# One form of d and the sum S4 moved one product later, and two blocks' rows normalised in other units

## The reference

```python
u = (x @ w_in).reshape(b, t, 4, 256)                  # four groups of 256 features
pooled[g] = trailing mean of u[:, :, g] over (2, 4, 8, 16)[g] rows
y = einsum('btgc,gce->btge', pooled - u, w_group) * scale
m = y @ w_out
h = layer_norm(ALPHA * x + m, ln_mix_g, ln_mix_b)
gate, up = split(h @ w_gu)                            # 2 x 2816 columns
h = layer_norm(ALPHA * h + (silu(gate) * up) @ w_down, ln_ffn_g, ln_ffn_b)
return h without the meta rows
```

## Time and profile before

| what | us |
|---|---|
| median of three executions | 1663.8 |
| the profiled execution | 1664.46 |
| its span | 1662.6 |
| TensorE busy in matmuls | 1643.4 |
| VectorE busy | 1040.2 |
| GpSimd busy | 649.1 |
| ScalarE busy | 616.8 |

### The profile page before, as it was taken

One profiled execution on the slowest core, in us unless ns is written; L12 is line 12 of the kernel. 1 busy time (PEld: TensorE's weight loads), 2 busy tenths in 40 slices (PEclk: granted clock), 3 DMA queues, 4 the chain that ended last, 5 costly groups with the idle time before them and its releaser, 6 DMA issues.

```text
span 1662.6 us, 19027 instructions
## 1 busy us (share of the span) xinstructions
PE 1643.4 (99%) x7302; PEld 1358.0 (82%) x7302; DVE 1040.2 (63%) x1085; ACT 616.8 (37%) x836; POOL 649.1 (39%) x440
## 2 busy tenths in 40 slices
PE   9999999999999999999999999999999999999998
PEld 7888888787788888888888888888888888888886
DVE  6788785987444544345756676676554434368866
ACT  5335465446333333433533333333333322222320
POOL 0330025015346767665356656666621000341002
PEclk9999999999999999999999999999999999999999
DMA  9774477535356566576556667666668443564542
GB/s 350 253 284 152 160 254 259 187 127 194 122 164 208 188 201 222 184 228 213 202 181 204 214 219 221 202 190 198 203 190 302 170 161 126 195 216 177 199 144 94
DMA packets 190954, 330.84 MB, mean 199 GB/s; under 512 B 8464, under 2 KB 132496, under 8 KB 181136
## 3 DMA queue, kind: packets, MB, share of 16 engines
q1 hardware_dynamic: 151168, 297.64, 52.3%
q10 hardware_dynamic: 37520, 23.60, 4.6%
q0 software_dynamic: 2176, 8.39, 1.3%
HBM read 227.36 MB, written 102.24 MB: 198 GB/s over the span
## 4 chain that ended last, share of the span: by engine, by line
PE 90%; DVE 3%; POOL 2%; DMA 2%; ACT 1%; issue 1%; SPq 0%; POOLq 0%; DVEq 0%; ACTq 0%
PE acc L1231 43%; PE acc L1260 19%; PE turn L1231 7%; PE acc L1066 7%; PE turn L1260 6%; PE acc L1100 5%; PE turn L1100 3%; DMA hf_dram<-ss_mix 1%; POOL ss_mix L885 1%; DMA raw<-w_out 1%; DVE split L1653 1%; DVE sums L1698 1%; PE acc L1143 1%; PE turn L1054 0%; POOL ss_mix L931 0%
## 5 line engine op out<-in xcount | busy, mean ns | idle before, releaser
L1231 PE MATMUL acc<-fa,wf 128*128 128x512 f32 x1584 | 369.5, 393 | 5.4 <-DVE acc L1951 4.0
L1231 PE MATMUL acc<-fb,wf 128*128 128x512 f32 x1584 | 363.2, 389 | 0.2 <-DVE acc L1951 0.2
L1231 PEld LDWEIGHTS acc<-fa,wf 128*128 128x128 f32 x1584 | 298.0, 189 | 68.4 <-DVE wf L1827 5.1
L1231 PEld LDWEIGHTS acc<-fb,wf 128*128 128x128 f32 x1584 | 297.1, 188 | 62.7 <-issue 1.1
L1260 PE MATMUL acc<-dw,da 128*128 128x512 f32 x1386 | 315.3, 389 | 0.0
L1260 PEld LDWEIGHTS acc<-dw,da 128*128 128x128 f32 x1386 | 260.1, 188 | 54.0
L1827 DVE TENSOR_TENSOR wf<-wt,wf 128x512 fp32r<-128x512 f32 x132 | 133.7, 1014 | 164.8 <-ACT wf L1432 164.7
L885 POOL TENSOR_TENSOR wt<-wr,wt 128x512 f32<-128x512 f32 x88 | 137.7, 1565 | 174.5 <-DVE wf L1827 174.5
L1827 DVE TENSOR_TENSOR wf<-wr,wf 128x512 fp32r<-128x512 f32 x176 | 171.8, 980 | 52.7 <-ACT wf L1432 52.2
L1432 ACT CAST wf<-wr 128x512 fp32r<-128x512 f32 x176 | 108.6, 618 | 214.1 <-PE acc L1231 208.6
L1066 PE MATMUL acc<-mov,split 128*128 128x512 f32 x768 | 177.5, 391 | 0.0
(11 more groups left out here) (139 smaller groups left out, 1807.1 us busy)
## 6 DMA issues: line engine op xcount, KB each, us to landing
wr<-w_gu SPq DMA_DIRECT2D x44, 1024.0 KB, 5.1
dar<-af_dram SPq DMA_DIRECT2D x56, 704.0 KB, 4.3
af_dram<-g ACTq DMA_DIRECT2D x32, 512.0 KB, 5.5
raw<-w_in SPq DMA_DIRECT2D x15, 1024.0 KB, 7.0
fs<-hf_dram SPq DMA_DIRECT2D x14, 1024.0 KB, 5.6
dt_raw<-w_down SPq DMA_DIRECT2D x22, 512.0 KB, 5.9
wt_dram<-dt_t SPq DMA_DIRECT2D x22, 512.0 KB, 3.6
sa<-af_dram SPq DMA_DIRECT2D x22, 512.0 KB, 8.0
```

Of the source, the lines that this page charges most:

```text
L1231: mm = nc.tensor.matmul(dst, wf[:, slot, a, k, :], fa[half][i][:, v, :, k, :], start=i < 2 and k == 0 and n3 == 0, stop=k == KC - 1 and n3 ...
```

## The change

Form 1 of d gets its low part (`d_lo(h, 1)`) behind the split of product 1's weights and no longer in chunk 2 of the half's second block. S4 is made once, over the full tile, in `d_sums(h, 3)`, and no longer in two halves, so that `sd_made` counts seven in a half. Two waits keep `d11` and `d12` until their forms' low parts are made. Of block 2, rows 2 and 3 are normalised in unit 0, behind the `s5` copy. Of block 3, rows 2 and 3 are normalised in unit 2, rows 0 and 1 in unit 3, and stored at n = 3 and 4 of SyncE's list. `load_tform(0, 0)` waits for the stores of rows 2 and 3 alone. `norm` waits for `shift_ready` at each call.

```diff
@@ -323,6 +323,9 @@
         def mov_of(b):
             return mov[b in (1, 2)]
 
+
+        LAST_ROWS = (2, 3, 0, 1)
+
         def raw_d(b, i):
 
             q = ((d11, d12), (d21, d22))[b % 2][i // 2]
@@ -333,7 +336,7 @@
 
         FORM_D = (d11, d12, d11, d21, d12, e3, d22)
 
-        FORM_SUMS = (0, 0, 7, 6, 8, 2, 0)
+        FORM_SUMS = (0, 0, 6, 5, 7, 2, 0)
         FORM_GROUPS = (2, 4, 0, 0, 0, 0, 8)
         A_BANK = (acc[:, 4, :], acc[:, 5, :], turn[:, 0, :], turn[:, 1, :])
         B_BANK = tuple(acc[:, m, :] for m in range(TT))
@@ -351,7 +354,7 @@
 
         def form_ready(eng, h, t):
             if FORM_SUMS[t]:
-                eng.wait_ge(sd_made, 8 * h + FORM_SUMS[t])
+                eng.wait_ge(sd_made, 7 * h + FORM_SUMS[t])
             else:
                 eng.wait_ge(d_ready, 2 * PAIRS * h + FORM_GROUPS[t])
 
@@ -502,7 +505,7 @@
                 sp.dma_start(zm[e][:, j, :], x_rows[:, b * TT + j, :]).then_inc(z_landed[e][j], 16)
 
             def store_h(b, j):
-                sp.wait_ge(normed, b * TT + (j + 1))
+                sp.wait_ge(normed, b * TT + (LAST_ROWS.index(j) if b == LAST else j) + 1)
                 sp.dma_start(h_rows[:, b * TT + j, :], zm[b % 2][:, j, :]).then_inc(rows_stored[b % 2][j], 16)
 
             def load_ft(k):
@@ -539,7 +542,7 @@
                     sp.wait_ge(tf_made[e], 4 * v)
                 elif e == 0:
 
-                    for j in range(TT):
+                    for j in LAST_ROWS[0:2]:
                         sp.wait_ge(rows_stored[1][j], 2 * 16)
                 else:
 
@@ -800,9 +803,9 @@
                     load_a22()
                 if n % 2 == 0 and jj - 1 >= JF:
                     store_s(jj - 1 - JF)
-                if n in (1, 2):
-                    store_h(LAST, 2 * (n - 1))
-                    store_h(LAST, 2 * (n - 1) + 1)
+                if n in (3, 4):
+                    for j in LAST_ROWS[2 * (n - 3):2 * (n - 2)]:
+                        store_h(LAST, j)
                 for e in range(2):
                     if n - 1 in TF_STEP[e]:
                         store_tform(e, TF_STEP[e][n - 1])
@@ -1408,7 +1411,7 @@
                 elif i == 2:
 
                     act.wait_ge(d_lo_ready, NP * LAST_HALF + 4)
-                    act.wait_ge(sd_made, 8 * (LAST_HALF + 1))
+                    act.wait_ge(sd_made, 7 * (LAST_HALF + 1))
                 elif i < 5:
                     act.wait_ge(d_lo_ready, NP * LAST_HALF + (6 if i == 3 else NP))
                 elif i == 5:
@@ -1433,8 +1436,7 @@
                                ).then_inc(wf_hi, 1)
 
             def norm(s, j):
-                if j == 0:
-                    act.wait_ge(shift_ready, s + 1)
+                act.wait_ge(shift_ready, s + 1)
                 zz = zm[s % 2][:, j, :]
                 nc.scalar.activation(zz, zz, ACT.Identity, bias=shift[:, j:j + 1],
                                      scale=rstd[:, j:j + 1]).then_inc(normed, 1)
@@ -1498,7 +1500,7 @@
                         for q in range(4):
                             unit_hi(0, q)
                     if t == NP - 1:
-                        for j in range(TT):
+                        for j in range(TT if h == 0 else 2):
                             norm(2 * h, j)
                     if h and t == NP - 1:
                         form_hi(5)
@@ -1586,9 +1588,12 @@
                 if n == ROW_UNIT0:
                     act.wait_ge(mgb_landed, 32)
                     nc.scalar.mul(mgb[:], mgb[:], ALPHA).then_inc(mgb_scaled, 1)
-                if n in (1, 2):
-                    norm(LAST, 2 * (n - 1))
-                    norm(LAST, 2 * (n - 1) + 1)
+                if n == 0:
+                    norm(LAST - 1, 2)
+                    norm(LAST - 1, 3)
+                if n in (2, 3):
+                    for j in LAST_ROWS[2 * (n - 2):2 * (n - 1)]:
+                        norm(LAST, j)
                 if turned_in(n)[0] is not None:
                     take_turn(turned_in(n)[0], turned_in(n)[1])
                 if n == 0:
@@ -1676,7 +1681,7 @@
                     dve.wait_ge(ft_made, 4 * KC)
                 if b == 2 and i == 0:
 
-                    dve.wait_ge(sd_made, 8)
+                    dve.wait_ge(sd_made, 7)
                 if b == 3 and i == 0:
 
                     dve.wait_ge(st_stored[0], 16 * TT // 2)
@@ -1716,12 +1721,17 @@
                 if i < 2:
                     nc.vector.tensor_tensor(e3[:, ks], d11[:, ks], d21[:, ks], ALU.subtract).then_inc(sd_made, 1)
                     return
-                at_ = 8 * h + 2 + 3 * (i - 2)
+                at_ = 7 * h + 2 + 2 * (i - 2)
                 nc.vector.tensor_tensor(d21[:, ks], d21[:, ks], d22[:, ks], ALU.add).then_inc(sd_made, 1)
                 dve.wait_ge(sd_made, at_ + 1)
+
+                dve.wait_ge(d_lo_ready, NP * h + 1)
                 nc.vector.tensor_tensor(d11[:, ks], d21[:, ks], d11[:, ks], ALU.subtract).then_inc(sd_made, 1)
-                dve.wait_ge(sd_made, at_ + 2)
-                nc.vector.tensor_tensor(d12[:, ks], d12[:, ks], d11[:, ks], ALU.subtract).then_inc(sd_made, 1)
+                if i == PAIRS - 1:
+                    dve.wait_ge(sd_made, at_ + 2)
+
+                    dve.wait_ge(d_lo_ready, NP * h + 2)
+                    nc.vector.tensor_tensor(d12[:], d12[:], d11[:], ALU.subtract).then_inc(sd_made, 1)
 
             def d_lo(h, t):
                 dve.wait_ge(d_hi_ready, NP * h + t + 1)
@@ -1849,8 +1859,8 @@
                         pool(b, i - 1)
                     elif b % 2:
                         pool(b - 1, PAIRS - 1)
-                    if b % 2 and i in (1, 2):
-                        d_lo(b // 2, i - 1)
+                    if b % 2 and i == 1:
+                        d_lo(b // 2, 0)
                     if b % 2 and i == 2:
                         d_sums(b // 2, 0)
                         d_sums(b // 2, 1)
@@ -1865,6 +1875,7 @@
                     if c < MIX_END:
                         split_lo(c, c % 2)
                     if t == 0:
+                        d_lo(h, 1)
                         pool(2 * h + 1, PAIRS - 1)
                         d_sums(h, PAIRS - 1)
                     if 1 <= t < NP - 1:
```

## The result

The changed kernel takes 1653.41 us (median of five, 1651.98 to 1654.94) against 1663.8 beside it; the ratio is 0.9936, with a 95% interval from 0.9923 to 0.9948. That is 10.4 us less; 12.2 were forecast. By the two spans, 1662.6 and 1651.6, it is 11.0.

What follows compares the result with a forecast made beforehand. TensorE, busy 99%, was taken to bound the kernel, with 13.22 us winnable at three stops. Gains of 4.0 + 1.05 + 7.14 = 12.2 us gave 1651.6 us against 1663.8, range 1650 to 1653.

Steps and rivals of the forecast that it cites:

- Stop A: TensorE's 3.13 us wait before the mixer's second half, plus 1.90 of half clock; 0.93 to stay, 4.0 won.
- The products after it: Mixer products after the second half's first: product 1 stops up to 0.1 us, product 2 fits by 0.3.
- Stop C: TensorE's 1.05 us wait before product 2 of unit 0, for ScalarE's bank copy; forecast gone, 1.05 won.
- Stop B: TensorE's 3.97 us wait before product 4 of unit 1, plus 3.17 of half clock; forecast gone, 7.14 won.
- VectorE as what is late next in unit 1: Before product 4 of unit 1: VectorE's sum done at 410.8, needed at 411.85, so it fits by 1.0 us.
- what the prediction feared of that operation: In unit 1, GpSimd's 1.47 us power operation could hold weight 2's low part, shrinking the cover from 1.0 to 0.1.
- The pair in units 2 and 3: Two tiles normalised in each unit ahead of the sum for product 4: cover 0.7 us, no stop, cost 0.
- SyncE and the DMAs: Row stores moved two units back; form load and pair read back still come in time, over 10 us remaining: cost 0.
- signs of being wrong: Stop over 1 us in second-half products 1-4, before unit 0's product 6 or units 1, 3's product 4; reduced clock after A.
- D: New stop of 1.03 us before product 6 of unit 4, found in the changed kernel; the prediction had none.
- the wider one: Range up to 1658.7 us, taking in the clock-or-tenths case and the case of a stop in B's place.
- the first rival: Mixer's second half: clock falls after A's rest or later products stop by tenths; 1.9 to 2.5 more, 1653.8 us; chance 0.16.

Runs made afterwards that it cites:

- The mixer's part alone: Against the kernel before: only form 1's low part moved and S4 made once over the full tile; rows, stores and waits as before: 1660.03 us, ratio 0.9974.
- four tiles in unit 2: Against the changed kernel: all four tiles of block 3 normalised in unit 2 behind the s5 copy, none in unit 3: 1655.51 us, timed once.
- e3's half moved: Against the kernel before: the second half of e3, one subtraction, put behind the split of product 0's weights: 1664.08 us, timed once.
- two tiles in unit 0: Against the kernel before: rows 2 and 3 of block 2 normalised in unit 0, nothing else of the change: 1661.97 us, ratio 0.9989.

## Why the prediction was right, and where not

- *Stop A.* Forecast 0.93 of stop left and the clock kept, 4.0 won. Measured 0.91, clock kept. From the moment TensorE was free to the start of unit 0 it took 381.39 - 299.85 = 81.54 before and 377.35 - 299.62 = 77.73 after: 3.8 won. The missing 0.2 is mostly a term that was too large: the half clock behind A was counted as 7.34 - 5.44 = 1.90, but 7.34 is the length of a row up to the end of its last matmul, and from start to start the 24 took 310.16 - 302.98 = 7.18, which is 1.74 over. The first matmuls behind the rest of the stop took 5.58 for 5.44, 0.1 more that wasn't counted, and the 0.1 that was counted for product 1 didn't come (0.02). The mixer's part alone gives 3.8 us too.
- *The products after it.* `d_lo(1, 2)` was done at 322.03 with product 2 at 322.45, so it fitted by 0.4, forecast 0.3; before it had fitted by 3.8 (322.72 for 326.48), not "by over 4".
- *The reason for the kept clock was wrong in part.* I argued from C, 1.05 us. The clock was kept at 0.91 and also at 1.71 in unit 2, but halved at 2.00 where 3.13 had halved it; my expectation for 2.0, which put it with C, failed. Whether between 1.71 and 2.00 the length or the place decides is open: the two are at different places.
- *Stop C.* Forecast gone, 1.05. Gone; the copy stood at 381.12, before the end of product 1 at 382.88.
- *Stop B.* Forecast gone, 7.14. Gone, with its half clock. From the start of unit 0 to product 4 of unit 1 it was 35.48 before and is 407.36 - 377.35 = 30.01 now, and the 3.0 of half clock come on top: 8.5 for C and B together against 8.19 forecast. The stops' idle times, 1.05 and 3.97, are 0.45 less than what TensorE lost in them from start to start (35.48 - 30.01 = 5.47), and the half clock, counted as 3.17 in the same way as A's, was 3.00.
- *VectorE as what is late next in unit 1.* Forecast cover 1.0 us, measured 0.7. VectorE's list was as forecast: the sum was done 406.63 - 377.35 = 29.28 us behind the start of unit 0, forecast 410.8 - 381.39 = 29.41. What came earlier is TensorE's need of it, 30.01 behind that start and not 411.85 - 381.39 = 30.46: the 0.45 of the bullet above. The Trainium skill, "SBUF — State Buffer", Who interferes with whom, has a VectorE operation with two SBUF inputs contend with a GpSimd operation that reads SBUF. Weight 1's low part agrees, with 1.78 us beside GpSimd's 1.67 from 403.21, and it was counted. Weight 2's low part doesn't: it took 0.68 us from 405.35 while GpSimd's power operation ran from 404.84 to 406.30, so that what the prediction feared of that operation did not come.
- *The pair in units 2 and 3.* Forecast cover 0.7, measured 0.6 in both; four tiles made the stop that this cover gives. The forecast took the row's length 14.05 where it is 13.88 from start to start; so counted, the cover was 0.5 before as well.
- *SyncE and the DMAs: the step that failed.* The prediction put the stores at "Cost 0". It followed those who wait for the moved stores (the load over their place, the pair read back) and not those who share the DMA engines with them. ScalarE's stores of gated rows, issued 4 us later, landed in up to 13.25 us and not in 5, and the buffer came free too late: 1.03 us of stop and 0.3 more from start to start. Moving the two stores 8 us ahead, counted from the start of unit 0, takes it away. The prediction also counted 5.3 us for a row store to land; the four of this stretch took 8.2 in the median, and the form load that waits for the first two was issued 9.9 us after the first of them. None of the rivals and none of the signs of being wrong has a stop before product 6 of unit 4.

The sum by stretches: 0.2 in the first 33 us, 3.8 + 8.5 - 1.3 = 11.0 behind them, together 11.2, against 11.0 by the spans; where the last 0.2 went, behind unit 4, isn't placed. The forecast of 12.2 was 1.3 too high by D. Most of the rest of the distance to 10.4 is that the profiled execution of before stood 0.66 over its median, as the prediction said, and the one of after on it.

The time, 1653.41, lies 0.4 over the forecast's own range (1650 to 1653) and inside the wider one. It is near the first rival's 1653.8, and that is chance: the clock was kept behind A and no product after it stopped. The forecast's mechanism is what happened, less D.

## What to carry to other kernels

When a transfer is moved, list what else is on the DMA engines in the microseconds it moves into, and which buffers wait for those landings, not only who waits for the moved one. A stop on a matmul engine is priced with the clock behind it, and one that is shortened but not below the length at which the clock was seen to be kept may give back nothing of that price (here from 3.13 us to 2.00). A stop is measured from start to start: its idle time was up to 0.3 us too little, and the length of a row of matmuls 0.16 too much. And when an engine's list is shortened, look for the next wait in it: the gap of 0.70 us was filled by changing the order of two steps.

## What the runs showed of the hardware that was not expected

The price of the half clock isn't fixed by the length of the stop. The last column is from start to start, over the full-clock time of the same matmuls. The one before it is how long the granted clock stood at 0.50, an estimate from its means in windows of 0.5 us:

| stop | kernel | length, us | at 0.50, us | half clock cost, us |
|---|---|---|---|---|
| A | after | 0.91 | none | 0.1 |
| product 4, unit 2 | four tiles in unit 2 | 1.71 | none | 0.1 |
| A | e3's half moved | 2.00 | 3.4 | 1.75 |
| A | before | 3.13 | 3.4 | 1.74 |
| B | before | 3.97 | 6.8 | 3.00 |
| B | the mixer's part alone | 3.97 | 6.8 | 2.79 |
| B | e3's half moved | 4.02 | 6.8 | 2.72 |
| B | two tiles in unit 0 | 4.52 | 3.4 | 1.61 |

The 0.1 of the first two rows is not half clock; it is there at full clock too. The longest stop cost the least of those that halved the clock. The price is about half of the time at 0.50 that lies behind the stop, for in it 8 matmuls ran in 3 us where 15 do at 1.00: (423.0 - 416.9) / 2 = 3.1 for B before, (417.8 - 414.7) / 2 = 1.6 for the longest. At A the price is 1.72 to 1.75 in all five kernels that halved there, so it is at B alone that it changed. The Trainium skill, "TensorE: Matmul & The Clock Gate", Part 1, calls the window in which the chip watches TensorE free-running. A price that changes from 3.00 to 1.61 at one place would fit that, but no run here shows the cause.
